# Head norms of a hybrid decoder layer: the first half's squares in two fp32r parts, and where ScalarE reads their sums

## The reference, cut to what matters

```
proj = h @ w_in                                     # split into q, k, v, gates of both groups
scores  = where(causal, q_rel @ k_rel.T, 0)         # per chunk; q_rel, k_rel scaled by exp(cum - mid)
o_intra = scores @ v
update  = k_to_end.T @ v                            # k_to_end = k * exp(cum_last - cum)
state_n+1 = decay_n * state_n + update_n
o = o_intra + (q * exp(cum)) @ state_n
o = o * rsqrt(mean(o * o, over the head) + eps) * gain * silu(gate)
x = x + gate1 * (o @ w_out);  then an MLP with squared ReLU;  final RMS norm
```

## Time and profile before

| | us |
|---|---|
| median of 3 runs (lowest to highest) | 1174.39 (1173.81 to 1174.96) |
| the profiled execution's own time | 1174.11 |
| its span | 1172.4 |
| PE (TensorE matmul) busy | 1153.4 |
| DVE (VectorE) busy | 808.7 |
| ACT (ScalarE) busy | 598.0 |
| POOL (GpSimd) busy | 445.2 |

### The profile page before, as it was taken

How to read it: one execution, slowest core, us unless ns; L and a number is a source line. 1 busy time by engine, 2 the same in 40 slices (tenths; PEclk the granted TensorE clock), 3 DMA queues, 4 the chain that set the end, 5 groups by cost and what they waited for, 6 DMA issues and landing times.

```text
span 1172.4 us, 15673 instructions
## 1 busy us (share of the span) xinstructions
PE 1153.4 (98%) x5651; PEld 956.8 (82%) x5651; DVE 808.7 (69%) x958; ACT 598.0 (51%) x899; POOL 445.2 (38%) x274
## 2 busy tenths in 40 slices
PE   7999999999999999999999999999999999999997
PEld 6778788888888888888888888888888888888886
DVE  6898766554536358357988755676796785966876
ACT  7763554646464647235655555455663443434325
POOL 1031111111111115326444442434367575666751
PEclk9999999999999999999999999999999999999999
DMA  9775241021111114351454435533723737437203
GB/s 352 261 233 162 90 145 36 19 55 36 36 36 36 37 37 144 90 162 72 117 171 162 158 120 171 178 132 130 226 72 119 253 96 252 153 126 279 90 1 144
DMA packets 148765, 152.02 MB, mean 130 GB/s; under 512 B 6228, under 2 KB 117976, under 8 KB 146008
## 3 DMA queue, kind: packets, MB, share of 16 engines
q1 hardware_dynamic: 148696, 151.12, 39.6%
HBM read 117.02 MB, written 34.08 MB: 129 GB/s over the span
## 4 chain that ended last, share of the span: by engine, by line
PE 89%; DVE 5%; issue 3%; DMA 1%; ACT 1%; SPq 1%; DVEq 0%; ACTq 0%
PE unit_bank L1338 29%; PE unit_bank L1640 9%; PE unit_bank L1642 9%; PE unit_bank L1641 9%; PE small_bank L1641 9%; PE small_bank L1640 9%; PE small_bank L1642 9%; PE small_bank L1338 3%; DVE ada_acc L1741 2%; PE small_bank L1473 2%; PE small_bank L1465 1%; PE small_bank L1377 1%; DMA ada_slot<-in_w_ada_dram 1%; DVE state L1941 1%; ACT a_hi L850 0%
## 5 line engine op out<-in xcount | busy, mean ns | idle before, releaser
L777 POOL TENSOR_TENSOR wr_lo<-quarter,wr_hi 128x512 fp32r<-128x512 f32 x122 | 195.8, 1617 | 174.9 <-ACT wr_hi L1130 174.8
L1338 PE MATMUL unit_bank<-a_hi,w_hi 128*128 128x512 f32 x560 | 223.3, 399 | 0.8 <-ACT t L957 0.8
L1338 PE MATMUL unit_bank<-a_hi,w_lo 128*128 128x512 f32 x560 | 218.4, 390 | 0.0
L1338 PE MATMUL unit_bank<-a_lo,w_hi 128*128 128x512 f32 x560 | 218.1, 389 | 0.0
L721 POOL TENSOR_TENSOR w_lo<-raw,w_hi 128x1024 fp32r<-128x1024 f32 x27 | 69.1, 2558 | 345.8 <-ACT w_hi L832 345.8
L1640 PE MATMUL unit_bank<-op_hi,wr_hi 128*128 128x512 f32 x452 | 176.5, 390 | 0.0
L1642 PE MATMUL unit_bank<-op_hi,wr_lo 128*128 128x512 f32 x452 | 175.9, 389 | 0.0
L1641 PE MATMUL unit_bank<-op_lo,wr_hi 128*128 128x512 f32 x452 | 175.9, 389 | 0.0
L1640 PE MATMUL small_bank<-op_hi,wr_hi 128*128 128x512 f32 x448 | 174.5, 390 | 0.0
L1641 PE MATMUL small_bank<-op_lo,wr_hi 128*128 128x512 f32 x448 | 174.3, 389 | 0.0
L1642 PE MATMUL small_bank<-op_hi,wr_lo 128*128 128x512 f32 x448 | 174.3, 389 | 0.0
(11 more groups left out here) (273 smaller groups left out, 1856.6 us busy)
## 6 DMA issues: line engine op xcount, KB each, us to landing
quarter<-in_w_mlp_dram SPq DMA_DIRECT2D x128, 256.0 KB, 4.5
hidden_scratch<-hid SPq DMA_DIRECT2D x98, 256.0 KB, 2.8
ada_slot<-in_w_ada_dram SPq DMA_DIRECT2D x48, 512.0 KB, 6.6
op_full<-hidden_scratch SPq DMA_DIRECT2D x21, 1024.0 KB, 4.8
raw<-in_w_in_dram SPq DMA_DIRECT2D x29, 512.0 KB, 3.6
raw<-in_w_out_dram SPq DMA_DIRECT2D x16, 512.0 KB, 4.0
x_stage<-in_x_dram SPq DMA_DIRECT2D x8, 512.0 KB, 5.8
x_scratch<-xT SPq DMA_DIRECT2D x2, 2048.0 KB, 8.3
```

The lines of the kernel that those rows point to most:

```text
L777: pool.tensor_tensor(wr_lo[slot][:, :, :], split_source(n), wr_hi[slot][:, :, :].bitcast(F32), ALU.subtract).then_inc(wr_lo_pool, 1)
L1338: return pe.matmul(out_ap, left, right, start=start, stop=stop)
```

## The change

The paired heads' squares of half 0 are split too. `sq_hi` of that half lies in a place of its own (`sq_hi_first`, the bytes of `ada_slot6`), all numbering of split products grows from 2 to 4 for a pair, and both halves use the same two fp32r products. ScalarE copies the high parts right behind the squares of slot 3, VectorE subtracts the low parts in slot 3 behind the two score tiles. ScalarE's `read_out(4)` moves, for pairs, ahead of `finished("k")` and the `k_end` exponential. Pieces 40 to 47 of `w_ada` get other places, and piece 41 waits for the head sums of P1's half 0.

```diff
     if kind == "split":
-        return (0, 0, 2)[gi] if isinstance(gi, int) and gi < 3 else 4 + 2 * (gi - 3)
+        return (0, 0, 4)[gi] if isinstance(gi, int) and gi < 3 else 8 + 2 * (gi - 3)
...
-    return half if prev == "H" else which if half == 1 else None
+    return half if prev == "H" else 2 * half + which
...
-... else (3, 6, 2)[n % 3]
+... else (3, 6, 2, 3, 2, 6, 3, 2, 6, 3, 2, 6)[n - 36]
...
+        sq_hi_first = at("sq_hi_first", 120, [P, 2, HALF], F32R)
...
+        def sq_high(prev, which, half):
+            return (sq_hi_first if prev == "P" and half == 0 else sq_hi)[:, which, :]
...
+                if n == 41:                                         # SyncE, load_ada
+                    sp.wait_ge(filled["ss"], 2)
...
-                    if splits and prev == "P":                      # ScalarE, read_out
-                        finished("o")
-                    for which, n in splits:
+                    for which, half, n in splits:
+                        if prev == "P" and half == 1:
+                            finished("o")
+                        if name == "P1" and half == 0:
+                            act.wait_ge(ada_added, 37 + 1)
                         act.wait_ge(o_squared, n + 1)
-                        act.activation(sq_hi[:, which, :], stat[:, which, :], ACT.Copy).then_inc(sq_hi_ready, 1)
+                        act.activation(sq_high(prev, which, half), stat[:, which, :], ACT.Copy).then_inc(sq_hi_ready, 1)
...
                 act.activation(k_rel[:, :], t0[:, :], ACT.Exp, scale=-sc).then_inc(e_k, 1)
+                if prev == "P":
+                    read_out(4)
                 finished("k")
                 act.wait_ge(d_last, gi + 1)
                 act.activation(k_end[:, :], t0[:, :], ACT.Exp, scale=-sc).then_inc(e_end, 1)
...
-                read_out(4)
+                if prev != "P":
+                    read_out(4)
...
-                        pe.wait_ge(o_squared, before("o", gi) + n + 1)      # TensorE, step, for half 0 of a pair
-                        mm = product(SB[b][:, :], ones[:, :], stat[:, which, :])
+                    pe.wait_ge(sq_lo_ready, before("split", gi) + split_number(prev, which, half) + 1)
+                    product(SB[b][:, :], ones_r[:, :], sq_high(prev, which, half), True, False)
+                    mm = product(SB[b][:, :], ones_r[:, :], sq_lo[:, which, :], False, True)
...
-                    for p in s[slot]:                               # VectorE, read_out
+                    for p in sorted(s[slot], key=lambda p: p[0] == "o"):
```

More of the change, by code:

```diff
@@ L246 @@
 ADA_PLAN = {"P0": [1, 0, 2, 0, 6, 0, 0, 4], "P1": [0, 0, 2, 2, 0, 2, 2, 2], "H0": [1, 1, 0, 0, 0, 0, 0, 0]}
-ADA_SLOT = [(0, 1, 2, 3, 4, 5, 7, 8)[n % 8] if n < 16 else n % 6 if n < 32 else (0, 1, 5, 2)[n - 32] if n < 36 else (3, 6, 2)[n % 3]
+ADA_SLOT = [(0, 1, 2, 3, 4, 5, 7, 8)[n % 8] if n < 16 else n % 6 if n < 32 else (0, 1, 5, 2)[n - 32] if n < 36 else (3, 6, 2, 3, 2, 6, 3, 2, 6, 3, 2, 6)[n - 36]
             for n in range(48)]
@@ L993, in read_out @@
                             act.activation(tok(row(mixed, head), half), src, ACT.Copy).then_inc(read["o"], 1)
-                            if split_number(prev, which, half) is not None:
-                                splits.append((which, n))
+                            splits.append((which, half, n))
                         elif kind == "ss":
@@ L1409, in step @@
                 else:
-                    at_n = split_number(prev, which, half)
-                    if at_n is None:
-                        pe.wait_ge(o_squared, before("o", gi) + n + 1)
-                        mm = product(SB[b][:, :], ones[:, :], stat[:, which, :])
[L1414 to L1417, removed]
+                    pe.wait_ge(sq_lo_ready, before("split", gi) + split_number(prev, which, half) + 1)
+                    product(SB[b][:, :], ones_r[:, :], sq_high(prev, which, half), True, False)
+                    mm = product(SB[b][:, :], ones_r[:, :], sq_lo[:, which, :], False, True)
                 mm.then_inc(filled[kind], 1)
@@ L1901, in read_out @@
                         if kind == "o":
[L1902 to L1906, removed]
+                            dve.wait_ge(sq_hi_ready, before("split", gi) + split_number(prev, which, half) + 1)
+                            dve.tensor_tensor(sq_lo[:, which, :], stat[:, which, :],
+                                              sq_high(prev, which, half).bitcast(F32), ALU.subtract).then_inc(sq_lo_ready, 1)
                         if kind not in ("up", "sc", "ss", "z"):
```

## The result

The changed kernel takes 1176.15 us (median of 18 runs, 1174.57 to 1178.55), the kernel before, run beside it, 1174.02 (18 runs, 1173.42 to 1176.01). The ratio is 1.0017, 95% interval 1.001 to 1.0023: slower by 2.1 us, less than 0.2%. The profiled execution's span is 1173.8 us; before it was 1172.4.

What follows compares the result with a forecast made beforehand. TensorE was taken as the bound, busy 1153.4 of 1172.4 us. P1's -0.80 and H0's +1.56 gave +0.76 on 1174.39, so 1175.15, about 1175.2 us; range 1172.9 to 1176.5.

Steps and rivals of the forecast that it cites:

- rival (c): TensorE's clock falls to its lower level behind the wait in H0, 1.7 us more: 1176.85 us; chance 0.08.
- the likeliest case: P1 -0.80, H0 +1.56, together +0.76 us: 1175.15, own range 1174.6 to 1176.1; chance 0.62.
- the main step: H0: moved sums make `k_end` 4.6 us later, so TensorE waits 2.36 us for state updates, against 0.80 saved.
- TensorE's saving: Half 0's head sums in P1 and H0: split products take 0.91 instead of 1.71 us, 0.80 a group, 1.6 in all.
- Copies and subtractions free: Slot 3: ScalarE's two added copies (1.04 us) and VectorE's two subtractions (1.30) cost TensorE nothing by themselves.
- The piece of SyncE: Piece 41 waits for P1's head sums, near 136.4 us, delaying the queue behind it; claimed free.
- H0's stop: TensorE waits 2.36 us at H0's slot 5 modulation transposes for VectorE's state updates, late behind `k_end`.
- P1's hold: GpSimd's subtraction holds VectorE's normalisations in P1 until 146.9 us; updates end at 150.6, 0.1 before TensorE; cost 0.
- Rival (b): GpSimd's hold of VectorE in P1 costs its full 0.9 us: 1176.1 us; chance 0.12.
- (a): No stop in H0, state updates ready in time, full saving of 1.6 us stays: 1172.8 us; chance 0.15.
- rival (d): One table load serves logarithm and exponential on ScalarE, everything behind 1.28 us earlier, sum -0.5: 1173.9 us; chance 0.03.
- the sum's last term: H0's +1.56 us: a TensorE wait of 2.36 at the transposes, with H0's own saving of 0.80 included.

Runs made afterwards that it cites:

- the better order: The changed kernel, but in H0 ScalarE makes the `k_end` exponential ahead of the head sums: 1172.56, 1173.98 and 1172.67 us, ratios 0.9987, 0.9999, 0.9989.

## Why the prediction was right, and where it was short

The time, 1176.15, lay in the range and within 0.2% of the kernel before, as forecast. That it did is in part luck. The change is +2.13 against a forecast of +0.76; rival (c), at +2.46 and with a chance of 0.08, was nearer. The range reached up to 1176.5, and 1176.15 is already above the likeliest case's own 1176.1. The kernel before was also 0.37 faster in the runs beside it than the 1174.39 from which the sum started; from there, +2.13 would have been 1176.52, just outside. The two parts of the main step, the saving and the stop, came as forecast.

- **TensorE's saving**, 0.80 a group: 0.83 in P1, and 1.66 in both. From P1's first sum to H0's updates 6 and 7 it is 204.31 - 134.88 = 69.43, before 206.68 - 135.59 = 71.09. With the better order 1.2 of it is left at the outputs.
- **Copies and subtractions free**: right. The piece of SyncE too: no new wait from there.
- **H0's stop**, reckoned 2.36 by a walk through ScalarE's and VectorE's instructions: 2.30, at the place, behind the engine and for the reason named. ScalarE's walk from the weights' copy to `k_end`: forecast 204.02 - 194.67 = 9.35, measured 202.48 - 193.13 = 9.35. The walk was exact because every duration in it was in the trace and no step of it could reorder.
- **P1's hold**: forecast to let the updates end 0.1 ahead of TensorE, measured 0.33. Rival (b) did not come, nor did (a).
- **One table load**, rival (d): no; there are two, each 1.28 long, and the next instruction starts 0.01 to 0.02 behind one. The Trainium skill (ScalarE: Activation LUTs, "What ACT_TABLE_LOAD costs") has a drain on top that no row here shows.
- **The step that was short** is the sum's last term, that the stop costs its own length alone. By the prediction's own sign (a clock below 1.00 near 210 us) rival (c) came in two of four profiles, and 1.6 us with it. The medians are 1.4 and 1.6 above +0.76, nearly a whole fall, which suggests that it came in more than half of the timed runs. The argument against it, that dense matmuls lie directly on both sides of the stop, did not hold, and the rows do not bear it out either: directly ahead lie the six small products of the updates (1.13), directly behind the eight transposes (207.74), and the dense unit starts at 209.12. The row at 28 us, a shorter standstill with small matmuls behind it, was the better guide. Whether the transposes have a part in the fall, no run here tells.

So the change bought 1.6 us of TensorE time and made a wait of 2.3 that in some executions costs 1.6 more. It relieved one hidden deadline (the sums' logarithm for updates 6 and 7, which in H0 had 0.3 us in hand: it ended at 205.11 + 1.26 = 206.37, TensorE came at 206.68) by breaking another (the state updates for the transposes, which had 3.1 us). The order that keeps both puts `k_end` first and the sums between it and tanh. It still pays 0.4 at a third one, the modulation rows for the outputs of half 1.

## What to carry to other kernels

When an in-order engine does several short jobs for a saturated one, each has a deadline: moving one job up by two table loads moves all others down, so walk every one of them to the instruction of the bound engine that needs it. A saving on the bound engine of a microsecond also brings all its deadlines forward by a microsecond. And price a new standstill of TensorE of two microseconds with the chance that the clock falls behind it; the trace's own earlier standstills say what that can cost. Where executions differ by more than the change is worth, compare the stretch that it touches, profile against profile.

## What the runs showed of the hardware

- The same 2.3 us standstill, between six small products and eight transposes, was followed by the lower clock for some 3 us in two profiles (0.51 and 0.64 in the mean over 4 us in one) and by full clock in two others of the same kernel (11.45 and 11.47 against 9.85 and 9.86 us for the same work). Filling 1.7 us of it with small matmuls took 1.6 us off the median.
- A VectorE instruction of four columns was held like a long one: `mod<-mod,cols` of 128x4, 0.16 us where GpSimd is idle, took 2.37 at 209.18 with the better order, where GpSimd's weight subtraction had begun at 209.14; both ended at about 211.5. The Trainium skill (SBUF — State Buffer, "SBUF: two separate sides") calls the shared port pair an exclusive lock for the whole instruction; the 2.37 agrees. TensorE waited 0.27 for the modulation row that came late by it.
